# Writing the stream between mixer and experts in the experts' column order, and moving the scratch zeroing and one copy of the last pair

## The reference, cut to what matters

```python
h = layer_norm(concat(meta, x), ln_in_g, ln_in_b)            # 16 + 256 tokens, 2048 columns
mix = mixer_stage(h, ...)        # MLA + retention, gated, merged, merged @ w_out
h = layer_norm(ALPHA * h + mix, ln1_g, ln1_b)                # the stream between mixer and experts
g_logits, e_logits = h @ w_group, h @ w_expert               # 4 groups, 32 experts
... top-1 group, top-2 experts inside it, weights e_w ...
ffn = sum over the two experts of e_w * (silu(h @ w1[e]) * (h @ w3[e])) @ w2[e]
out = layer_norm(ALPHA * h + ffn, ln2_g, ln2_b)[:, 16:]
```

## Time and profile before

| | us |
|---|---|
| median of 3 runs | 2144.16 (2141.87 to 2147.51) |
| the profiled execution | 2139.88 |
| its span | 2138.1 |
| PE, DVE, ACT busy | 2073.6, 1585.6, 1285.5 |
| TensorE clock granted, mean | 0.995 |

### The profile page before, as it was taken

The page is one execution under the profiler, slowest core; times in us unless marked ns, Lnnn a source line. Parts: engine busy times, 40 slices in busy tenths (PEclk is TensorE's granted clock), DMA queues, the critical chain, the costliest instruction groups (busy, mean ns, idle before and its releaser), DMA issues.

```text
span 2138.1 us, 30052 instructions
## 1 busy us (share of the span) xinstructions
PE 2073.6 (97%) x11484; PEld 1752.5 (82%) x11484; DVE 1585.6 (74%) x1417; ACT 1285.5 (60%) x1064; POOL 102.9 (5%) x75
## 2 busy tenths in 40 slices
PE   8999999999999999999999999999999999999996
PEld 8998888899999998887887777877777787778763
DVE  7646554453646465455669999999999999999997
ACT  5435663333233323334247888888888888888883
POOL 1000000000000000001000000000000000000000
PEclk9999999999999999999999999999999999999998
DMA  6556545655454544656757999999999999999994
GB/s 214 153 139 186 154 138 177 203 184 170 157 173 143 175 152 143 196 193 241 229 232 293 403 420 422 420 422 421 419 421 417 421 419 417 417 416 417 420 409 202
DMA packets 172703, 606.47 MB, mean 284 GB/s; under 512 B 20251, under 2 KB 36779, under 8 KB 121547
## 3 DMA queue, kind: packets, MB, share of 16 engines
q1 hardware_dynamic: 169072, 598.01, 74.0%
q0 software_dynamic: 3552, 7.37, 1.1%
HBM read 595.05 MB, written 22.04 MB: 289 GB/s over the span
## 4 chain that ended last, share of the span: by engine, by line
PE 67%; DVE 16%; issue 8%; DMA 6%; ACT 3%; DVEq 0%; POOLq 0%; SPq 0%; POOL 0%; ACTq 0%
PE ps L1935 19%; PE ps L1916 15%; DVE wl L740 11%; PE ps L1072 6%; PE ps L1073 6%; DMA raw<-in_w_dram 6%; PE ps L2286 4%; PE ps L1069 4%; PE ps L1094 2%; ACT wh L590 2%; PE ps L2041 2%; PE ps L2021 2%; PE ps L1042 1%; DVE yall L904 1%; PE ps L2008 1%
## 5 line engine op out<-in xcount | busy, mean ns | idle before, releaser
L740 DVE TENSOR_TENSOR wl<-raw,wh 128x2048 fp32r<-128x2048 f32 x351 | 789.3, 2287 | 44.2 <-ACT wh L590 42.7
L590 ACT ACTIVATE wh<-raw 128x2048 fp32r<-128x2048 f32 x351 | 668.6, 1915 | 133.3 <-DMA raw<-in_w_dram 67.3
L1504 DVE TENSOR_TENSOR wl<-raw,wh 128x2048 fp32r<-128x2048 f32 (+1 forms) x168 | 379.9, 2263 | 285.6 <-ACT wh L1306 285.5
L1306 ACT ACTIVATE wh<-raw 128x2048 fp32r<-128x2048 f32 (+1 forms) x168 | 317.9, 1894 | 444.9 <-DMA raw<-in_w_in_dram 279.7
L1072 PE MATMUL ps<-wh,xg 128*128 128x512 f32 x896 | 373.2, 416 | 24.0 <-DVE wl L740 23.4
L1073 PE MATMUL ps<-wl,xg 128*128 128x512 f32 x896 | 351.6, 392 | 0.0
L1916 PE MATMUL ps<-hth,wh 128*128 128x272 f32 (+1 forms) x896 | 259.7, 290 | 3.2 <-DVE wl L1504 1.8
L1916 PE MATMUL ps<-htl,wh 128*128 128x272 f32 (+1 forms) x896 | 255.8, 285 | 0.0
L1916 PE MATMUL ps<-hth,wl 128*128 128x272 f32 (+1 forms) x896 | 255.6, 285 | 0.0
L1072 PEld LDWEIGHTS ps<-wh,xg 128*128 128x128 f32 x896 | 169.1, 189 | 76.0 <-DVE wl L740 27.4
L1072 PE MATMUL ps<-wh,hx 128*128 128x512 f32 x508 | 202.9, 399 | 1.4 <-issue 1.4
(11 more groups left out here) (368 smaller groups left out, 3065.8 us busy)
## 6 DMA issues: line engine op xcount, KB each, us to landing
raw<-in_w_dram SPq DMA_DIRECT2D x384, 1024.0 KB, 10.1
raw<-in_w_in_dram SPq DMA_DIRECT2D x103, 1024.0 KB, 5.1
raw<-in_w_pa_dram SPq DMA_DIRECT2D x16, 1024.0 KB, 5.0
raw<-in_w_pb_dram SPq DMA_DIRECT2D x16, 1024.0 KB, 5.0
raw<-in_w_out_dram SPq DMA_DIRECT2D x16, 1024.0 KB, 5.0
raw<-in_w_ukv_dram SPq DMA_DIRECT2D x8, 1024.0 KB, 5.4
yscr<-zeros SPq DMA_DIRECT2D x4, 1024.0 KB, 9.9
yrow<-yscr SPq DMA_DIRECT2D x4, 1024.0 KB, 8.2
```

Source lines behind the costliest of these rows:

```text
L590: nc.scalar.activation(wh2[:, x % HELD, :], raw2[:, slot2(x), :], ACT.Copy).then_inc(s_wh2, 1)
L740: nc.vector.tensor_tensor(wl2[:, slot2(x), :], raw2[:, slot2(x), :], wh2[:, x % HELD, :].bitcast(F32), ALU.subtract).then_inc(s_wl2, 1)
L1306: nc.scalar.activation(wh[:, n % RING1, 0:c], raw1[:, n % RING1, 0:c], ACT.Copy).then_inc(s_wh, 1)
L1504: nc.vector.tensor_tensor(wl[:, n % RING1, 0:c], raw1[:, n % RING1, 0:c], wh[:, n % RING1, 0:c].bitcast(F32), ALU.subtract).then_inc(s_wl, 1)
```

## The change

1. `copy_out` writes `mrg` with columns reordered to k*128+p. It reads the residual and the PSUM banks 16 floats apart and writes runs of 32 floats. `turn_stream(j)` waits for all eight operations of `copy_out`, since a block of 128 columns now holds parts of all j. `xh1` and `xl1` read `mrg` without a stride. The router's weights, `g1t` and `b1t` follow the same order. The scale and shift of the first normalisation are reordered by two DRAM-to-DRAM copies in pieces of 4 bytes into a new scratch `lscr`, issued on POOL ahead of its wait for `s_m`, and are loaded from there.
2. The zeroing of `yscr` leaves the gate loop. `zeros` becomes 256 columns wide and is cleared by POOL behind `s_h1`; SP writes the four quarters, in pieces of 1 KB instead of 512 B, just ahead of `ln2g`. Each expert's `product` on DVE waits for `s_zs`.
3. The copies to `evens` move from steps 10 (high) and 17 (low) to 10 (high) and 1 (low).
4. Each `yrow` load waits for its own unit (16 to 19) of the last pair, and POOL no longer waits for unit 19 ahead of `s_all`.

```diff
-        zeros = place("zeros", [P, P], 203904)
+        zeros = place("zeros", [P, 4 * SLOTS], M0 + 5120)
+        lscr = nc.dram_tensor("lscr", (2, D_MODEL), F32).ap()
...
                     if n == RING2:
+                        sp.wait_ge(s_zt, 1)
+                        for r in range(SCRATCH_ROWS // P):
+                            sp.dma_start(yscr[P * r:P * (r + 1), :].rearrange("p (b c) -> p b c", c=4 * SLOTS),
+                                         zeros[:, :].unsqueeze(1).broadcast_to([P, KD // 2, 4 * SLOTS])).then_inc(s_zs, 16)
                         sp.wait_ge(s_h1, TT)
...
                     for r in range(2):
+                        if isinstance(turn, int):
+                            done(sp, turn + PAIRS - 1, 16 + 2 * t + r)
                         sp.dma_start(yrow[:, t, r, :],
...
+            for v, src in enumerate((ins["ln1_g"], ins["ln1_b"])):
+                pool.dma_start(lscr[v:v + 1, :].rearrange("a (k p) -> (a k) p", k=KD),
+                               src.rearrange("a (p k) -> (a k) p", k=KD), allow_slow_non_contiguous=True).then_inc(s_ls, 16)
             pool.wait_ge(s_m, 9)
...
+            pool.wait_ge(s_h1, TT)
+            nc.gpsimd.memset(zeros[:, :], 0.0).then_inc(s_zt, 1)
             pool.wait_ge(s_zs, 16 * (SCRATCH_ROWS // P))
...
-                pool.wait_ge(s_used2, 24 * PAIRS * rounds - 4)
+                if not isinstance(rounds, int):
+                    pool.wait_ge(s_used2, 24 * PAIRS * rounds - 4)
...
-                    if k in (10, 17) and last:
-                        nc.scalar.activation(evens[k == 17][:, :].rearrange("q (p k) -> q k p", k=KD),
+                    if k in (1, 10) and last:
+                        nc.scalar.activation(evens[k == 1][:, :].rearrange("q (p k) -> q k p", k=KD),
...
-                nc.scalar.activation(xh1[:, t, :, :], mrg[:, t, :].rearrange("q (p k) -> q k p", k=KD),
+                nc.scalar.activation(xh1[:, t, :, :], mrg[:, t, :].rearrange("q (k p) -> q k p", k=KD),
...
-                nc.vector.tensor_tensor(xl1[:, t, :, :], mrg[:, t, :].rearrange("q (p k) -> q k p", k=KD),
+                nc.vector.tensor_tensor(xl1[:, t, :, :], mrg[:, t, :].rearrange("q (k p) -> q k p", k=KD),
...
             def product(j, par, before_):
+                dve.wait_ge(s_zs, 16 * (SCRATCH_ROWS // P))
...
-                sp.dma_start(yscr[bass.ds(P * i - P, P), :].rearrange("p (b c) -> p b c", c=P),
-                             zeros[:, :].unsqueeze(1).broadcast_to([P, KD, P])).then_inc(s_zs, 16)
...
-                    nc.vector.scalar_tensor_tensor(mrg[:, t, c], xr[:, t, c], ALPHA, ps[:, 2 * j + t, :], ALU.mult,
+                    nc.vector.scalar_tensor_tensor(mrg[:, t, :].rearrange("q (k p) -> q k p", k=KD)[:, :, 32 * j:32 * (j + 1)],
+                                                   xr[:, t, c].rearrange("q (p k) -> q k p", k=KD), ALPHA,
+                                                   ps[:, 2 * j + t, :].rearrange("q (p k) -> q k p", k=KD), ALU.mult,
                                                    ALU.add).then_inc(s_co, 1)
...
-                pe.wait_ge(s_co, 2 * j + 2)
+                pe.wait_ge(s_co, 2 * TT * 2)
```

More of the change, by code:

```diff
@@ L354, in moe_trunk @@
         gscr = nc.dram_tensor("gscr", (2, D_MODEL), F32).ap()
+        lscr = nc.dram_tensor("lscr", (2, D_MODEL), F32).ap()
         yscr = nc.dram_tensor("yscr", (SCRATCH_ROWS, D_MODEL), F32).ap()
         s_c2 = sem("s_c2")
+        s_ls = sem("s_ls")
         s_tok = sem("s_tok")
@@ L531, in stage_constants @@
         def stage_constants(pool):
+            for v, src in enumerate((ins["ln1_g"], ins["ln1_b"])):
+                pool.dma_start(lscr[v:v + 1, :].rearrange("a (k p) -> (a k) p", k=KD),
+                               src.rearrange("a (p k) -> (a k) p", k=KD), allow_slow_non_contiguous=True).then_inc(s_ls, 16)
             pool.wait_ge(s_m, 9)
[L534 to L537, removed]
+            pool.wait_ge(s_ls, 32)
+            for dst, src in ((ln1g[:, :], lscr[0:1, :].broadcast_to([P, D_MODEL])),
+                             (ln1b[:, :], lscr[1:2, :].broadcast_to([P, D_MODEL])),
+                             (wr[:, :, 0:N_GROUPS], ins["w_group"][0].rearrange("(p k) n -> p k n", p=P)),
+                             (wr[:, :, N_GROUPS:], ins["w_expert"][0].rearrange("(p k) n -> p k n", p=P)),
                              (brt[:, 0:N_GROUPS], ins["b_group"].broadcast_to([P, N_GROUPS])),
@@ L543, in stage_constants @@
             for dst, src in ((g1t, ins["ln1_g"]), (b1t, ins["ln1_b"])):
-                pool.dma_start(dst[:, :], src.rearrange("a (k p) -> p (a k)", p=P),
-                               allow_slow_non_contiguous=True).then_inc(s_c2, 16)
+                pool.dma_start(dst[:, :], src.rearrange("a (p k) -> p (a k)", p=P)).then_inc(s_c2, 16)
             nc.gpsimd.iota(tokm[:, :], [[P, TT]], -OUTSIDE, 1,
@@ L659, in pair @@
                         nc.scalar.activation(selt[:, :], ps[:, 7, 0:SEQ], ACT.Copy, scale=1.0 / ALPHA).then_inc(s_stc, 1)
-                    if k in (10, 17) and last:
-                        nc.scalar.activation(evens[k == 17][:, :].rearrange("q (p k) -> q k p", k=KD),
-                                             (xh1, xl1)[k == 17][:, 1, :, :].bitcast(F32), ACT.Copy).then_inc(s_own, 1)
+                    if k in (1, 10) and last:
+                        nc.scalar.activation(evens[k == 1][:, :].rearrange("q (p k) -> q k p", k=KD),
+                                             (xh1, xl1)[k == 1][:, 1, :, :].bitcast(F32), ACT.Copy).then_inc(s_own, 1)
                     for q in range(8):
@@ L1269, in _ @@
                     sp.dma_start(dst[:, :, to:to + width], src[:, :, at:at + width]).then_inc(s_raw[n % RING1], 16)
-            sp.wait_ge(s_zt, 1)
             with sp.Fori(1, 4 + 1) as i:
                 job(N_GA, i - 1, w_in, C_GA + 512 * i - 512)
-                sp.dma_start(yscr[bass.ds(P * i - P, P), :].rearrange("p (b c) -> p b c", c=P),
-                             zeros[:, :].unsqueeze(1).broadcast_to([P, KD, P])).then_inc(s_zs, 16)
             with sp.Fori(1, 4 + 1) as i:
@@ L1507, in _ @@
             nc.vector.memset(half[:, :], -0.5).then_inc(s_half, 1)
-            nc.vector.memset(zeros[:, :], 0.0).then_inc(s_zt, 1)
             for c, s in enumerate((s_oa, s_ob, s_g, s_m)):
@@ L1836, in copy_out @@
                     dve.wait_ge(s_co, 2 * j + t + 1)
-                    s = nc.vector.bn_stats(bst[:, t, j, :], mrg[:, t, c])
+                    s = nc.vector.bn_stats(bst[:, t, j, :],
+                                           mrg[:, t, :].rearrange("q (k p) -> q k p", k=KD)[:, :, 32 * j:32 * (j + 1)])
                 own.after(s)
@@ L1843, in router_sums @@
                 dve.wait_ge(s_c2, 16 * 12)
-                dve.wait_ge(s_zs, 16 * (SCRATCH_ROWS // P))
                 for c, v in ((1, b1t), (0, g1t)):
```

## The result

The changed kernel took 2166.14 us (2164.29 to 2169.02), the kernel before in the same comparison 2144.44: ratio 1.0102, 95% interval 1.0087 to 1.0116, 21.7 us slower. The forecast was 2143.3, the range 2136 to 2151. The spans of the profiled executions lie 27.0 us apart, 2165.1 against the 2138.1 of the earlier trace rows: the execution of before (2139.88) lay 4.6 us under the median of this comparison, that of after (2166.97) 0.8 us over its own.

What follows compares the result with a forecast made beforehand. The expert loop was taken as bound by weight loads at 420 GB/s. Terms -0.85 + 2.4 + 0 - 2.1 - 0.3 = -0.85 us, on the median of 2144.16, gave 2143.3 us; range 2136 to 2151.

Steps and rivals of the forecast that it cites:

- The order of the scale and shift: Copies to `lscr` beside projection weight loads: cost 0, up to one landing of 9.8 us without cover.
- what would show the prediction wrong: Signs listed beforehand, among them PE waiting at the projection for a load late behind the `lscr` copies.
- three units of PE work ahead: Projection stage: loads are issued this far ahead of use, so delays from the copies cost 0.
- Rival D: Ahead of load 8, zero writes take their landing time, 9.9 us each, ending 23 us late: 2166; chance 0.08.
- Gate units: First gate units: without the zero write a load comes sooner, -0.85 us (0 to -1.4).
- Hand-over: Mixer to experts: transposes wait for all evacuations, which get slower by strided reads, +2.4 us (1.6 to 3.1).
- an earlier `xl1` finds PE in its own queue: Hand-over: PE is held by gathers and warm matmuls, so a shorter `xl1` saves 0, at best -2.9 us.
- Rival A: Hand-over: the clock falls in PE's new gap, 1.7 us more, 2145.0; chance 0.18.
- Zeroing in its new place: Behind `s_h1`, ahead of load 8: zeros are done in time, cost 0 (0 to +1.7 us).
- Last pair: Copies to `evens` moved: -4.7 us for the stall ahead of `mix`, +2.6 at step 1, net -2.1.
- rival B: Last pair: the copy at step 1 is absorbed, 2.6 us less, 2140.7; chance 0.14.
- End: After the last loads: earlier `yrow` lets DVE do its first sum before `last_rest`, -0.3 us.

Runs made afterwards that it cites:

- e1: The changed kernel without the two copies to `lscr`, scale and shift loaded in natural order: 2139.33 us, ratio 0.9979.
- e2: The kernel before plus only the two DRAM-to-DRAM copies and POOL's wait for them: 2173.17 us, ratio 1.0129.
- e8: e4 with the zeroing, its tile and its waits put back behind the first four gate loads: 2142.07 us, ratio 0.9990.
- e9: e4 with fewer warm matmuls ahead of the two parts of `xl1` (one each instead of 3 and 8): 2137.51 us, ratio 0.9972.
- e4: The changed kernel with the 4-byte pieces gathered into SBUF and written to `lscr` in rows of 512 B: 2138.98 us, ratio 0.9979.
- e3: The changed kernel with the copy of the scale alone, the shift loaded in natural order: 2143.60 us, ratio 1.0002.
- e10: The changed kernel with the second copy issued 170 us later, behind the wait for the branches: 2153.0 us, ratio 1.0050.
- e6: The kernel before with everything of the change but the column order, so without copies: 2136.10 us, ratio 0.9959.
- e11: e4 with 8 warm matmuls in the new gap at the hand-over: 2138.42 us, ratio 0.9980.
- e12: e4 with the edits of both e9 and e11: 2135.20 us, ratio 0.9963.
- e7: e4 with the copies to `evens` put back at steps 10 and 17: 2144.0 us, ratio 1.0001.
- e5: The changed kernel with both DRAM-to-DRAM copies in natural order, 32 rows of 512 B: 2140.56 us, measured once.

## Why the prediction was wrong

**The order of the scale and shift: the step that failed.** It put 0 on the copies, and at most one landing of 9.8 us. They cost 26.8 us between the medians (after against e1), 28.9 alone on the kernel before (e2). Two things were wrong in it.

First the price. 9.8 us was the landing of `g1t`, whose 4-byte pieces end in SBUF: the right number of pieces, the wrong destination. It was no price of such pieces either, since it stood in a burst of twelve constants, among them two of 1 MB. Another of them, of 32 KB, took as long in the kernel before:

```profile
fold<-in_fold_dram POOLq DMA_DIRECT2D x1, 32.0 KB, 9.5
```

A copy whose pieces are written to DRAM took 12.5 us, and the second 25 us more, beside loads that crawled at 74 to 229 GB/s.

Second the cover: "three units of PE work ahead" was not turned into microseconds. It lasted 17 us. Against it stand the 38.3 us of the load's landing and the 4.4 of its two parts on ACT and DVE, and the difference is PE's wait of 25.5. With two landings of 9.8, one behind the other, the same sum gives a wait of some 10 us: an estimate, from 19.6 for the copies less the 2 by which they were ahead, 5.0 for the load, 4.4 for its parts, less 17. So the cover in microseconds would have shown a risk, and only the right price its size. The list of what would show the prediction wrong did hold this very wait of PE.

**Rival D** gave 2166 and the result is 2166.1, but by chance: its mechanism did not occur. The zeros landed in 8.8 us at the median, overlapping, before load 8.

**Gate units.** Forecast -0.85. PE's idle fell by 0.93 us, so the term was right for the profile. Undone, it costs 2.4 to 3.1 us (e8): the gap of 2.0 us there lowered the clock, and the one of 0.9 did in no profile. The first 190 us were 1.0 us shorter besides, by PE's first transposes, which took 6.23 us in after, 7.30 in before and between 6.1 and 7.4 in the others: no part of the change.

**Hand-over.** Forecast +2.4. The two evacuations take 1.92 us against 1.28; the median of all eight is 1026 ns against 680, so one payment of 0.35 each, as taken, though both inputs are read 16 floats apart. (The Trainium skill, SBUF — State Buffer, Door 1, gives PSUM lines of 8 bytes and says that accesses which are not contiguous there slow matmuls. The prediction carried this over to VectorE's read, for 3.1 us; the row is against that.) From the first possible transpose to unit 0 it took 31.7 us, before 29.8: +1.95. The claim that an earlier `xl1` finds PE in its own queue is shown by e9, where unit 0 comes 1.9 us sooner by a shorter queue (1.5 between the medians).

**Rival A, the clock in the new gap,** did not come true in the profile of after, and did in six of the nine profiles with this gap of 2.09 us; in e4, where the transposes took 5.38 us, the term is +3.6, not +2.4. So A is no rival that is true or false of the gap alone: the same gap went both ways. What decides it is not shown; the three profiles without the fall (after, e3, e10) are those in which PE had waited near 860. The 3 to 4 us between e6 and e4 have it in them. Yet e11, which fills the gap, was only 0.6 us faster at the median than e4; in e12, against e9, it is 2.3.

**Zeroing in its new place.** Forecast 0 to +1.7, taken 0; measured 0, load 8 standing as far behind unit 0 as before. The remark that a row is against the rule of 512 B was weak: it set 4.55 us for a zero write, found beside a load, against 2.50 for a load in the full stream, while one load by itself took 3.35.

**Last pair.** Forecast -2.1: -4.7 and +2.6. The +2.6 was right (2.5 in e4 against e7), so rival B was wrong. From load 8 to the first matmul that adds the stream back (`stream_back`, lines 1168 and 1183) before needs 974.6 us, after 973.9: -0.7 in these profiles. Up to PE's wait of 2.68 us it is +2.9. Behind it -3.6 and not -4.7: the stall of 2.97 us is gone, PE is busy for 1.3 us less, and a new wait of 0.6 for `lo` has come. At the median the move brought 5.0 us (e7). The clock's loss behind the stall ahead of `mix` was 1.7 us in the profile of before, 3.4 in e2 and 5.1 in e7, and the trace of before had shown the cheap one. That this spread makes up the 5.0 is likely and not shown.

**End.** Forecast -0.3. From the same matmul to the end it takes 30.26 us, before 31.01: -0.75, nearly the 0.8 that DVE's earlier sum could give.

**The sum.** For the profiled executions -1.9 at the gate and ahead of it, +28.3 for the copies, +1.95, -0.7 and -0.75 make +26.9 of the 27.0. Without the copies that is -1.4, near the -0.85 of the forecast, while the medians say -5 (e1, e4). Most of the difference is the choice of executions: that of before lay 4.6 us under its median and that of after 0.8 over, 5.4 together. Carrying the forecast over to the median held only if the terms cost there what they cost in a fast execution. Executions differ in which gaps lose clock, and for how long, and the change takes two such places away (gate, `mix`) and adds one. That fits, but was not tested.

## What to carry to other kernels

Cost a DMA by its number of pieces, their size and the side on which they are small; a row with another destination is no price, and a permutation into DRAM is better gathered into SBUF and written in rows. Turn every "it is covered" into microseconds of work queued in front of the waiting engine, and hold that against the sum of what is issued together. Where PE will idle for about as long as the gaps after which the clock sometimes fell (here 2.0 to 3.0 us), cost it as a chance with its portions, and fill it with warm matmuls, or take them out where they stand in the way of real work.

## What the runs showed of the hardware

Two copies of 8 KB from DRAM to DRAM in 4-byte pieces kept the DMA engines at a recorded share of 0.5 to 1.2 for 20 us at 0 to 10 GB/s (in e2, from 840 to 860, 0.2 to 1.0 at 1 to 3 GB/s); the same pieces into SBUF took 5.3 and 6.7 us, and the same bytes from DRAM to DRAM in rows of 512 B 2.0 and 1.9.

The clock's losses come in portions. Summed over windows of 4 us in all fourteen profiles, a gap ahead of the output stage, the 25 us of the copies apart, cost 0, 1.7 or 5.1 us, and 3.4 in three cases. Two windows behind e4's gap in the last pair, then the same place in e5:

```profile
2070.00:2074.00 4.00, 4.00 (x19) 3.71 (x17) 3.14 (x3) 3.32 (x2) 0.00 (x0) 0.50 1.02 414
2074.00:2078.00 4.00, 4.00 (x14) 3.42 (x15) 3.55 (x7) 0.38 (x1) 0.47 (x1) 0.50 0.62 254
```

```profile
2070.00:2074.00 4.00, 4.00 (x21) 3.69 (x20) 3.16 (x3) 3.47 (x2) 0.00 (x0) 0.60 1.02 414
2074.00:2078.00 4.00, 4.00 (x17) 2.71 (x17) 3.60 (x7) 1.84 (x2) 0.44 (x1) 1.00 0.77 285
```

The wait ahead of both was 2.7 us. That is 3.4 us, and with it the spans 2141.9 and 2138.7. The gap of 2.69 us behind the gates lowered the clock in eight profiles and left it full in six (e4, e5, e7, e9, e11, e12); with one profile of each kernel it stays open whether the kernel or the execution decides that. e12, whose profile shows no loss ahead of the output stage (span 2133.3), is the one kernel whose runs, five of them, lie within 0.4 us of each other. That these portions make most of the 7 us spread of the kernel before fits these numbers, but it was not tested.
